# A hybrid mLSTM / gMLP layer on one core: the second pair of output projection tiles as seven block products, with the work around it moved between engines

## Chip, cores and metric

The kernel runs on one core of a Trainium2 chip. The metric is device time in microseconds (us) of one execution. One execution is also profiled; its span, from the first to the last instruction, is the clock of all rows below.

## The reference, cut to what matters

There is one layer. The token count is 520: 512 of a prompt and 8 single tokens of samples. The model width is 1024 and the hidden width 2816.

```
xn = rmsnorm(x, g1);  z = xn @ w_in                  # q, k, v, o, gates, u, vb, ga, gb
y_a = (sigmoid(o) * mlstm(q, k, v, ig, lf)) @ w_a    # recurrence over 4 chunks of 128 tokens, 4 heads
y_b = spatial_gate(gelu(u), rmsnorm(gelu(vb))) @ w_b
merged = sigmoid(ga) * y_a + sigmoid(gb) * y_b
x = x + merged @ w_o                                 # x1: the output projection, called WO here
xn = rmsnorm(x, g2)                                  # needs the sum of x1's squares
up = xn @ w_up;  conv over 3 rows;  x = x + (silu(a) * gval) @ w_down;  rmsnorm(x, g_final)
```

## The kernel before, in words

**Tiles and slots.** Activations lie feature-major: 128 features on the partitions, 520 tokens in the row, `KT` = 8 feature blocks. A weight slot is 1024 by 128, which gives one output tile of 128 features. Slots are numbered in the order in which they are used; `S_WO` is the first of the 8 slots of the output projection, `S_UP` follows, then `S_DN`. Two buffers of each kind (`raw`, `whi`, `wlo`, and the output banks `out_ps`) are used by even and odd slots in turn.

**Each product is made of three.** Every fp32 operand is split in a high part, which fp32r holds exactly, and a low part, the rest. For a weight slot SyncE loads `raw`, ScalarE copies it to `whi` (`split`, line 581 through the helper `A`), VectorE subtracts to get `wlo` (`low`, L1083), and TensorE multiplies whi by x high, whi by x low and wlo by x high. With 8 blocks of the inner dimension and two halves of 260 tokens (`HALF`) that is 48 matmuls a slot. `split` of slot c waits until slot c-2 is done, since it overwrites that slot's `whi`.

**Seven products for eight.** In some places two output tiles are calculated as a 2 by 2 block product: two inner halves, two halves of the tokens. Seven products of 12 matmuls each (`product`) take the place of eight. This needs sums of weight blocks (`weight_sums`, lines 1497 to 1502: four VectorE operations in two dependent steps), seven factors split by `factor_hi` on ScalarE and `factor_low` on VectorE (L1491), and four combinations of the activations (0 to 3), split the same way (`x_combination_hi` on ScalarE, `x_combination_low` on VectorE, L1430). The factors are, in order, a11, a12, wsum3, wsum1, wsum0, wsum2, a22, so the third product (number 2, after 0 and 1) is the first that needs the weight sums. Before the change five pairs of gate tiles (`pairs_w`) and three pairs of the down projection (`pairs_d`) do this. In the gate pairs the first four factors of the next pair are prepared while two ordinary tiles (`n2`, `n3`) run between pairs. The combinations of x for the gate pairs are made by VectorE with `x_sum` (L1421) and `x_difference` (L1425): two of the sums in the last two steps of the recurrence (m = 6 and 7), the rest right behind it.

**The output projection.** After the last gate pair, 8 tiles follow, `S_WO` to `S_WO + 7`. For each, VectorE adds the residual `xres` (L1605, one operand in PSUM) to get `x1[j]`, ScalarE makes `x2h`, VectorE `x2l` (L1610). GpSimd loads `xres` and the convolution's constants by DMA, prepares the samples' share of the convolution (`sconv`, lines 1926 to 1931, behind a DMA that writes `conv_old`), and then squares each `x1[j]` (L1936) and adds it to `acc` (L1938). TensorE sums `acc` over the partitions (`norm_sums`) in the midst of tile `S_UP`, after its sixth of eight steps.

**Order.** Each engine runs its own list of instructions in the order in which they are written. Nothing reorders them. Waits are on semaphores, and a waiting instruction holds up all behind it on its engine.

Of the kernel before, what the change touches and what calls it, by code (L numbers as in the profile page):

```python
# [86 lines left out]
def hybrid_layer(nc, ins, outs):  # L87
    with ExitStack() as ctx:
# [92 lines left out]
        assert 16800 + 3 * NH * DVA * 4 >= XB + 3 * XB // 4  # L181
        acth = at("acth", [P, FT, TOK], Q0, F32R)
# [54 lines left out]
        sqa = st("sqa", [P, TOK], 2080)  # L237

# [55 lines left out]
        class DownPair(Pair):  # L294


            def __init__(self, i):
                self.q = GATE_PAIRS + i
# [14 lines left out]
        pairs_d = [DownPair(i) for i in range(DOWN_PAIRS)]  # L313
        pairs_w = [Pair(q) for q in range(GATE_PAIRS)]
# [104 lines left out]
        s_dc = sem("down_product_copied")  # L419
        s_nh = sem("branch_half_hi")  # L420
# [4 lines left out]
        s_acc = sem("norm2_sums")  # L425
        s_ss2 = sem("norm2_broadcast")
# [39 lines left out]
        def _(sp):  # L466
# [70 lines left out]
            load_slots(S_WO, S_DN)  # L537
# [41 lines left out]
        def _(act):  # L579
# [280 lines left out]

            def next_factors_hi(pr):
# [27 lines left out]
            def ay_pair(pr):  # L889
# [28 lines left out]
                if last:  # L918
                    split(At(S_WO + 1))
                else:  # L920
# [10 lines left out]
            with act.Fori(0, KT // 2) as i:  # L931
                for t in range(2):
                    n = At(S_WO + t, i, 2)
                    split(n.plus(2))
                    apart()
                    act.wait_ge(s_x1, i * 2 + (t + 1))
                    A(x2h[:, i * 2 + t, :], x1[:, i * 2 + t, :], scale=gains[:, 2, bass.ds(i * 2 + t, 1)]).then_inc(s_x2h, 1)


# [44 lines left out]
            def down_combination_hi(r, src, at):  # L984

                act.wait_ge(s_bt, 4 + at)
# [89 lines left out]
        def _(dve):  # L1076
# [378 lines left out]
            for m in range(2 * NC):  # L1455
# [12 lines left out]
                unit_denominator(2 * m + 1)  # L1468
                if m == 6:
                    x_sum(0, 0, 0)  # L1470
                if m == 7:
                    x_sum(1, 0, 1)
# [30 lines left out]

            def first_gate_sum(pr):
# [38 lines left out]
            def ay_pair(pr):  # L1543
# [28 lines left out]
                if last:  # L1572
                    low(At(S_WO))
                    merged_low(pr.j)
# [24 lines left out]
            def wo_step(i):  # L1599

                for t in range(2):
                    n = At(S_WO + t, i, 2)
                    j = i * 2 + t
                    ready(n)
                    TT(both(x1[:, j, :]), out2(n), both(xres[:, j, :]), ALU.add).then_inc(evac[n.c % 2], 1)  # L1605
                    dve.drain()
                    dve.nop().then_inc(s_x1, 1)
                    low(n.plus(2))
                    dve.wait_ge(s_x2h, i * 2 + (t + 1))
                    STT(x2l[:, j, :], x1[:, j, :], gains[:, 2, bass.ds(j, 1)], x2h[:, j, :].bitcast(F32),  # L1610
                        ALU.mult, ALU.subtract).then_inc(s_x2, 1)

            dve.wait_ge(s_xres, 16)
            wo_step(0)
            dve.wait_ge(s_xrest, 16)
            with dve.Fori(1, KT // 2) as i:
                wo_step(i)
# [82 lines left out]
            def down_combination_low(r, src, at):  # L1700

                dve.wait_ge(s_th, 4 + at)
# [121 lines left out]
        def _(pool):  # L1824
# [93 lines left out]
            pool.dma_start(xres[:, 2:KT, :], ins["x_all"][:, 2:KT, :]).then_inc(s_xrest, 16)  # L1918
            pool.wait_ge(done, S_WO + 1)
            pool.dma_start(cst[:, :, :, :], ins["conv_state"]).then_inc(s_ffl, 16)  # L1920
            pool.dma_start(cwb[:, :, :], ins["conv_wb"]).then_inc(s_ffl, 16)
            pool.wait_ge(s_ffl, 32)
# [9 lines left out]
            pool.memset(acc[:, :], 0.0)  # L1932
            pool.drain()
            for j in range(KT):
                pool.wait_ge(s_x1, j + 1)
                pool.tensor_tensor(sqa[:, :], x1[:, j, :], x1[:, j, :], ALU.mult)  # L1936
                pool.drain()  # L1937
                pool.tensor_tensor(acc[:, :], acc[:, :], sqa[:, :], ALU.add)  # L1938
                pool.drain()  # L1939
# [19 lines left out]
        def _(pe):  # L1959
# [254 lines left out]
            def branch_tile(pr, hi, lo):  # L2214
# [14 lines left out]
            for pr in pairs_w:  # L2229
# [4 lines left out]
                branch_tile(pr, *branches)  # L2234
# [4 lines left out]
            with pe.Fori(1, 4) as i:  # L2239
                for t in range(2):  # L2240
                    tile(At(S_WO + t, i, 2), mh, ml)
# [51 lines left out]
            def down_pair(pr):  # L2293
# [12 lines left out]
                pe.wait_ge(s_tl, 4 + 2)  # L2306
                product(pr, 3, pr.p6, *down_combination(2)).then_inc(s_pd, 1)
                product(pr, 4, pr.p5, *down_combination(0)).then_inc(s_pd, 1)
                pe.wait_ge(s_tl, 4 + 3)
                product(pr, 5, pr.p7, *down_combination(1)).then_inc(s_pd, 1)  # L2310
                pe.wait_ge(s_tl, 4 + 4)
# [137 lines left out]
```

## Time and profile before

| | |
|---|---|
| median of 3 runs | 898.91 us (898.21 to 899.29) |
| the profiled execution | 898.24 us, its span 896.4 us |
| granted TensorE clock, mean | 0.997 of full |
| TensorE matmul busy | 887.7 us, 99% |
| VectorE / ScalarE / GpSimd busy | 68% / 44% / 15% |

TensorE is busy nearly all the time, so what it does sets the time. The other engines prepare its operands. Their shares are averages; what matters is whether each operand is ready when TensorE comes to it.

### The profile page before, as it was taken

To read this page: it belongs to the slowest core of one execution; us is meant where nothing else is said; L and a number is where in the kernel's file an instruction comes from. 1 tells how busy PE (TensorE), PEld (TensorE's weight loads), DVE (VectorE), ACT (ScalarE), POOL (GpSimd) and SP (SyncE) were. 2 spreads that over 40 slices of the span, in tenths; PEclk is the share of its full clock that TensorE was granted. 3 is DMA by queue.
4 is the path that set the end of the run, shared out by engine and by line. 5 is a ranking of instruction groups with operands and counts; after the bars stand their busy time and mean duration, and the time that the engine had idled before them with its cause. 6 is when DMAs were issued, how large, how long until landed. Compare 5 with 4: busy or idle time off the path is not lost.

```text
span 896.4 us, 18963 instructions
## 1 busy us (share of the span) xinstructions
PE 887.7 (99%) x7306; PEld 883.2 (99%) x7306; DVE 609.7 (68%) x980; ACT 390.5 (44%) x629; POOL 133.0 (15%) x182
## 2 busy tenths in 40 slices
PE   9999999999999999999999999999999999999997
PEld 8999999999999999999999999999999999999997
DVE  7895775442885568677755777777777778966544
ACT  7535434544864334344432344444444444433334
POOL 0673000002542110000005700000000000000001
PEclk9999999999999999999999999999999999999998
DMA  6332253234872222322255222222222222333232
GB/s 214 114 123 94 72 202 99 78 99 155 280 269 72 71 72 75 115 95 94 95 200 136 83 82 94 94 94 94 94 88 82 87 94 88 99 107 88 89 106 96
DMA packets 31499, 100.44 MB, mean 112 GB/s; under 512 B 4668, under 2 KB 7260, under 8 KB 31192
## 3 DMA queue, kind: packets, MB, share of 16 engines
q1 hardware_dynamic: 29256, 92.96, 31.2%
q0 software_dynamic: 1472, 5.72, 2.2%
q10 hardware_dynamic: 720, 1.04, 0.4%
q8 instruction: 36, 0.59, 0.3%
q14 instruction: 15, 0.12, 0.0%
HBM read 92.37 MB, written 7.35 MB: 111 GB/s over the span
## 4 chain that ended last, share of the span: by engine, by line
PE 88%; issue 3%; POOLq 3%; DMA 2%; DVE 2%; POOL 1%; ACT 0%; DVEq 0%; SPq 0%; ACTq 0%
PE out L1961 81%; PE trp L1961 3%; PE aux L1961 2%; POOLq L1939 2%; POOLq L1937 1%; DMA raw_pair<-in_w_slots 1%; PE trp L1995 1%; DMA cwb<-in_conv_wb 1%; PE aux L2153 0%; DVE wlo L1083 0%; DVE tf L1425 0%; DVE tl L1430 0%; POOL y L1952 0%; DVE tf L1421 0%; POOL out_conv_old L1923 0%
## 5 line engine op out<-in xcount | busy, mean ns | idle before, releaser
L581 ACT ACTIVATE whi<-raw_pair 128x1024 fp32r<-128x1024 f32 (+4 forms) x168 | 154.2, 924 | 210.3 <-PE out L1961 196.4
L1083 DVE TENSOR_TENSOR wlo<-raw_pair,whi 128x1024 fp32r<-128x1024 f32 (+1 forms) x121 | 154.0, 1273 | 89.6 <-ACT whi L581 89.2
L1961 PE MATMUL out<-xh,whi 128*128 128x260 f32 x668 | 143.4, 289 | 0.4 <-DVE wlo L1491 0.4
L1961 PE MATMUL out<-x2h,wlo 128*128 128x260 f32 x704 | 141.9, 283 | 0.0
L1961 PE MATMUL out<-x2h,whi 128*128 128x260 f32 x704 | 141.8, 282 | 0.0
L1961 PE MATMUL out<-x2l,whi 128*128 128x260 f32 x704 | 141.7, 283 | 0.0
L1961 PE MATMUL out<-xl,whi 128*128 128x260 f32 x668 | 139.3, 283 | 0.0
L1961 PE MATMUL out<-xh,wlo 128*128 128x260 f32 x668 | 139.2, 283 | 0.0
L1961 PEld LDWEIGHTS out<-x2h,whi 128*128 128x128 f32 x704 | 108.6, 188 | 0.1
L1961 PEld LDWEIGHTS out<-x2h,wlo 128*128 128x128 f32 x704 | 108.5, 188 | 0.0
L1961 PEld LDWEIGHTS out<-x2l,whi 128*128 128x128 f32 x704 | 108.2, 188 | 0.0
L1961 PEld LDWEIGHTS out<-xh,whi 128*128 128x128 f32 x668 | 105.4, 189 | 1.0 <-issue 0.6
L1961 PEld LDWEIGHTS out<-xh,wlo 128*128 128x128 f32 x668 | 105.0, 188 | 0.0
L1961 PEld LDWEIGHTS out<-xl,whi 128*128 128x128 f32 x668 | 104.9, 188 | 0.0
L1961 PE MATMUL out<-acth,whi 128*128 128x260 f32 (+2 forms) x266 | 58.2, 283 | 0.0
L1961 PE MATMUL out<-acth,wlo 128*128 128x260 f32 (+2 forms) x266 | 58.0, 283 | 0.0
L1961 PE MATMUL out<-actl,whi 128*128 128x260 f32 (+2 forms) x266 | 57.9, 283 | 0.0
L1645 DVE TENSOR_TENSOR up<-out,rbc 128x520 f32<-128x520 f32 x44 | 30.8, 701 | 38.9 <-PE out L1961 38.8
L1945 POOL COPY nconv<-up 128x10 f32 x44 | 10.4, 236 | 241.4 <-DVEq L1646 241.4
L581 ACT ACTIVATE acth<-silu 128x520 f32 (+1 forms) x22 | 14.1, 639 | 69.8 <-DVE silu L1660 69.8
L1961 PEld LDWEIGHTS out<-acth,whi 128*128 128x128 f32 x266 | 42.8, 188 | 0.1
L1961 PEld LDWEIGHTS out<-acth,wlo 128*128 128x128 f32 x266 | 42.8, 188 | 0.0
(362 smaller groups left out, 1755.8 us busy)
## 6 DMA issues: line engine op xcount, KB each, us to landing
raw_pair<-in_w_slots SPq DMA_DIRECT2D x123, 512.0 KB, 3.3
raw_pair<-in_w_dn SPq DMA_DIRECT2D x16, 448.0 KB, 3.4
c_ring<-in_C_state SPq DMA_DIRECT2D x8, 512.0 KB, 5.4
row<-scratch SPq DMA_DIRECT2D x8, 512.0 KB, 5.7
out_C_sample<-c_ring SPq DMA_DIRECT2D x8, 512.0 KB, 4.9
raw_pair<-in_w_dn SPq DMA_DIRECT2D x8, 512.0 KB, 3.5
xres<-in_x_all POOLq DMA_DIRECT2D x1, 1560.0 KB, 6.9
x<-in_x_all SPq DMA_DIRECT2D x5, 260.0 KB, 6.8
```

Of the source, the lines that this page charges most:

```text
L581: return act.activation(out, in_, func, **kw_)
L1083: TT(wlo[p][:, 0:width], raw[p][:, 0:width], whi[p][:, 0:width].bitcast(F32), ALU.subtract)\
L1645: TT(both(up[t][:, 2:2 + TOK]), out2(n), both(rbc2[:, :]), ALU.mult).then_inc(evac[n.c % 2], 1)
L1937: pool.drain()
L1939: pool.drain()
L1945: pool.tensor_copy(nconv[:, i * 2 + t, :], up[t][:, SEQ:2 + TOK]).then_inc(s_nc, 1)
L1961: return pe.matmul(*a, **k)
L1995: m = pe.transpose(trp[b.c % 2][:, c, :], ftmp[b.c % 2][:, c * P:(c + 1) * P], ident[:, :])
```

## The change

1. **OutPair.** Output tiles `j` = 2 and 3 become a pair of seven products, between tile `S_WO + 1` and tile `S_WO + 4`. Its slot `S_WO + 4` is loaded and split in halves, as a gate pair's third slot is. The four combinations are of `merged`, whose last two of eight tiles come from the last gate pair.
2. **x's combinations** move: the sums to steps 4, 5 and 6 of the recurrence, three differences to steps 6 and 7.
3. **Squares** of x1 are made by ScalarE (`second_square`) into two buffers in turn; GpSimd only adds them. A square waits until the square two before it has been added.
4. **GpSimd's conv preparation** comes behind the first four additions, ahead of the last four.

The diff, cut to its core (the gpsimd block is told whole; the DMA order and the buffers are left out where they only follow):

```diff
@@ VectorE, in the recurrence
+                if m == 4: x_sum(0, 0, 0)
+                if m == 5: x_sum(1, 0, 1)
                 if m == 6:
-                    x_sum(0, 0, 0)
+                    x_sum(2, KT // 2, 1)
+                    x_difference(0, 1, 0)
                 if m == 7:
-                    x_sum(1, 0, 1)
+                    x_difference(1, 2, 1)
+                    x_difference(2, 2, 0)
@@ VectorE, behind the recurrence (by_plain, i == NC)
-                    x_difference(0, 1, 0)
                     unit_low(NC * NH - 1)
-                    x_sum(2, KT // 2, 1)
-                    dve.drain()
-                    x_difference(1, 2, 1)
-                    x_difference(2, 2, 0)
@@ VectorE, last gate pair
                     low(At(S_WO))
+                    merged_difference(0, merged_quarter(0, 1), merged_quarter(0, 0))
                     merged_low(pr.j)
@@ VectorE, the output projection (wo_step for all j before)
+            def out_pair(pr):
+                ready(At(S_WO)); first_sum(At(S_WO), 0); first_result()
+                merged_combination_low(0, 1)
+                merged_combination_low(2, 2)
+                factor_low(pr, 0)
+                factor_low(pr, 1)
+                weight_sums(pr)
+                ready(At(S_WO + 1)); first_sum(At(S_WO + 1), 1); first_result()
+                factor_low(pr, 2)
+                second_low(0)
+                factor_low(pr, 3)
+                merged_combination_low(1, 3)
+                factor_low(pr, 4)
+                factor_low(pr, 5)
+                merged_combination_low(3, 4)
+                second_low(1)
+                dve.wait_ge(s_xrest, 16); dve.wait_ge(s_pd, 6 * q + 3)
+                first_sum(n[0], j)
+                factor_low(pr, 6)
+                ...
+                TT(part(0, 1), part(0, 1), wtmp[1], ALU.add)
+                first_result()
+                low(n[3])
+                ready(n[1])
+                TT(part(1, 0), rest(0), wtmp[0], ALU.add)
+                TT(part(1, 1), rest(1), wtmp[0], ALU.add)
+                dve.drain()
+                TT(part(1, 0), part(1, 0), out_ps[pr.t1][:, 0, 0:HALF], ALU.add).then_inc(evac[pr.t1], 1)
+                ...
+            dve.drain()
+            merged_difference(2, merged_quarter(1, 1), tf[:, 0, :, :])
+            merged_difference(1, merged_quarter(1, 1), merged_quarter(0, 1))
+            dve.drain()
+            merged_difference(3, merged_quarter(1, 0), tf[:, 2, :, :])
+            out_pair(pair_o)
@@ ScalarE
+            def second_square(j):
+                act.wait_ge(s_x1a, j + 1)
+                A((ftmp[1], ftmp2)[j % 2][:, :], x1[:, j, :], ACT.Square).then_inc(s_x1q, 1)
+            def out_pair(pr):
+                factor_hi(pr, 0); factor_hi(pr, 1)
+                second_hi(0); second_square(0)
+                act.wait_ge(s_sw, 4 * q + 4); act.wait_ge(done, n[1]())
+                factor_hi(pr, 2); factor_hi(pr, 3)
+                ...
+                split(n[3])
+                second_square(1)
+            merged_combination_hi(2, 2); merged_combination_hi(1, 3); merged_combination_hi(3, 4)
+            out_pair(pair_o)
+            second_hi(2); second_square(2); second_hi(3); second_square(3)
+            for j in range(4, KT):
+                split(At(S_WO + j + 2)); second_hi(j); second_square(j)
@@ SyncE
-            load_slots(S_WO, S_DN)
+            load_slots(S_WO, S_WO + 4)
+            (S_WO + 4 once the pair's weight sums and two low factors are made, S_WO + 5 once all seven are)
+            load_slots(S_WO + 6, S_DN)
@@ GpSimd
+            pool.memset(acc[:, :], 0.0); pool.drain()
+            for j in range(4): square_added(j)      # wait for the square, acc += square, drain
             (DMA of conv_old, four tensor operations of the conv preparation)
-            for j in range(KT): (wait for x1[j], sqa = x1 * x1, drain, acc += sqa, drain)
+            for j in range(4, KT): square_added(j)
@@ TensorE
-            with pe.Fori(1, 4) as i:  (tiles S_WO + 2 to S_WO + 7)
+            out_pair(pair_o)                        # products 0 to 6, 12 matmuls each
+            halves_tile(pair_o, mh, ml)             # S_WO + 4
+            for j in range(5, KT): tile(At(S_WO + j), mh, ml)
```

## Rows read from the trace of the kernel before

**Rows 1.** The page, busy time of the engines.
```profile
PE 887.7 (99%) x7306; PEld 883.2 (99%) x7306; DVE 609.7 (68%) x980; ACT 390.5 (44%) x629; POOL 133.0 (15%) x182
```
**Rows 2.** The chain that ended last: start, us, what.
```profile
46.71 5.77 PE out L1961 x48
...
349.21 4.76 DMA raw_pair<-in_w_slots
```
**Rows 3.** Timeline of TensorE: start, us, line, operation, count, idle before.
```profile
357.87 0.28 PE L1961 MATMUL out<-xh,wlo 128*128 128x260 f32 x1
358.52 0.35 PE L1961 MATMUL out<-xh,whi 128*128 128x260 f32 x1 [0.37 <-DVE wlo L1491]
...
463.72 0.40 PE L1961 MATMUL out<-mh,whi 128*128 128x260 f32 x2
...
475.25 0.40 PE L1961 MATMUL out<-mh,whi 128*128 128x260 f32 x2
```
**Rows 4.** Timeline of VectorE: a combination, the weight sums, two factors.
```profile
342.58 1.24 DVE L1430 TENSOR_TENSOR tl<-tf,th 128x1040 fp32r<-128x1040 f32 x1
...
373.66 0.68 DVE L1497 TENSOR_TENSOR wsum<-raw_pair 128x512 f32<-128x512 f32 x1
...
375.82 0.69 DVE L1502 TENSOR_TENSOR wsum<-raw_pair,wsum 128x512 f32<-128x512 f32 x1
...
378.16 1.29 DVE L1491 TENSOR_TENSOR wlo<-wsum,whi 128x512 fp32r<-128x512 f32 x2
```
**Rows 5.** Timeline of ScalarE: a combination's high part, two factors, mh, x2h.
```profile
337.61 1.08 ACT L581 ACTIVATE th<-tf 128x1040 fp32r<-128x1040 f32 x1 [2.47 <-DVE tf L1425]
...
377.49 1.15 ACT L581 ACTIVATE whi<-wsum 128x512 fp32r<-128x512 f32 x2 [4.55 <-PE out L1961]
...
465.44 0.64 ACT L581 ACTIVATE mh<-merged 128x520 fp32r<-128x520 f32 x1 [0.40 <-DVE merged L1481]
...
470.75 0.73 ACT L581 ACTIVATE x2h<-x,gains  x1
```
**Rows 6.** Timeline of VectorE at the start of the output projection.
```profile
465.33 1.22 DVE L1083 TENSOR_TENSOR wlo<-raw_pair,whi 128x1024 fp32r<-128x1024 f32 x1
466.46 0.69 DVE L1486 TENSOR_TENSOR ml<-merged,mh 128x520 fp32r<-128x520 f32 x1
469.75 0.70 DVE L1605 TENSOR_TENSOR x<-out,xres 128x520 f32<-128x520 f32 x1 [2.60 <-PE out L1961]
...
471.93 0.75 DVE L1610 SCALAR_TENSOR_TENSOR x2l<-x,gains,x2h 128x520 fp32r<-128x520 f32 x1
```
**Rows 7.** Timeline of VectorE and GpSimd together, 487 to 492 us.
```profile
487.43 1.32 POOL L1938 TENSOR_TENSOR acc<-acc,sqa 128x520 f32<-128x520 f32 x1
488.08 1.74 DVE L1083 TENSOR_TENSOR wlo<-raw_pair,whi 128x1024 fp32r<-128x1024 f32 x1 [0.27 <-ACT whi L581]
...
488.88 1.85 POOL L1936 TENSOR_TENSOR sqa<-x 128x520 f32<-128x520 f32 x1
489.75 1.55 DVE L1610 SCALAR_TENSOR_TENSOR x2l<-x,gains,x2h  x1
```
**Rows 8.** Weight loads of the output projection (SyncE), time from issue to landing.
```profile
DMA to landing us min/median/max: 3.1/3.3/6.7
```
**Rows 9.** Timeline of GpSimd: the convolution's preparation, and the last sum of squares.
```profile
473.41 2.07 POOL L1923 DMA_DIRECT2D out_conv_old<-cst  x1 [7.63 <-DMA cwb<-in_conv_wb]
...
483.18 1.07 POOL L1929 TENSOR_TENSOR sconv<-sconv,cwb 128x352 f32<-128x352 f32 x1 [6.01 <-issue]
484.41 1.21 POOL L1931 TENSOR_TENSOR sconv<-sconv,sct 128x352 f32<-128x352 f32 x1
...
512.20 2.11 POOL L1938 TENSOR_TENSOR acc<-acc,sqa 128x520 f32<-128x520 f32 x1
```
**Rows 10.** Timeline of TensorE around the sum over the partitions in tile S_UP.
```profile
513.93 0.41 PE L1961 MATMUL out<-x2h,wlo 128*128 128x260 f32 x2
514.41 1.14 PE L1961 MATMUL aux<-acc,ones 128*128 128x260 f32 x4
```

More of the change, by code:

```diff
@@ L313, in hybrid_layer, with __init__ @@
         pairs_d = [DownPair(i) for i in range(DOWN_PAIRS)]
+        class OutPair(Pair):
+            def __init__(self):
+                self.q = GATE_PAIRS
+                self.j = 2
+                self.n = [At(S_WO + 2 + t) for t in range(4)]
+                self.t0, self.t1 = self.n[0].c % 2, self.n[1].c % 2
+                self.p1, self.p6 = (trp[t][:, :, :].rearrange("p a b -> p (a b)")[:, 0:HALF] for t in range(2))
+                self.p5, self.p7 = (aux[:, t, 0:HALF] for t in range(2))
+                r0, r1 = raw[self.t0], raw[self.t1]
+                self.a11, self.a12, self.a21, self.a22 = r0[:, 0:HW], r0[:, HW:], r1[:, 0:HW], r1[:, HW:]
+                self.factor = (self.a11, self.a12, wsum[:, 3, :], wsum[:, 1, :], wsum[:, 0, :], wsum[:, 2, :], self.a22)
+        pair_o = OutPair()
+        wtmp = (ftmp[0][:, 0:HALF], ftmp[0][:, HALF:TOK])
         pairs_w = [Pair(q) for q in range(GATE_PAIRS)]
@@ L425, in hybrid_layer @@
         s_acc = sem("norm2_sums")
+        s_x1q = sem("x1_squared")
+        s_x1a = sem("x1_squares_summed")
         s_ss2 = sem("norm2_broadcast")
@@ L928, in _, with second_hi @@
                 ay_pair(pr)
[L931 to L937, printed above, removed]
+            def second_hi(j):
+                act.wait_ge(s_x1, j + 1)
+                A(x2h[:, j, :], x1[:, j, :], scale=gains[:, 2, j:j + 1]).then_inc(s_x2h, 1)
@@ L940, in up_step @@
+            merged_combination_hi(2, 2)
+            merged_combination_hi(1, 3)
+            merged_combination_hi(3, 4)
+            out_pair(pair_o)
+            second_hi(2)
+            second_square(2)
+            second_hi(3)
+            second_square(3)
+            for j in range(4, KT):
+                split(At(S_WO + j + 2))
+                second_hi(j)
+                second_square(j)
             def up_step(i, first=False, last=False):
@@ L1597, in _ @@
                 ay_pair(pr)
[L1599 to L1611, printed above, removed]
@@ L1613, in _, with second_low, first_sum @@
-            dve.wait_ge(s_xres, 16)
[L1614 to L1617, printed above, removed]
+            def second_low(j):
+                dve.wait_ge(s_x2h, j + 1)
+                STT(x2l[:, j, :], x1[:, j, :], gains[:, 2, j:j + 1], x2h[:, j, :].bitcast(F32),
+                    ALU.mult, ALU.subtract).then_inc(s_x2, 1)
+            def first_sum(n, j):
+                return TT(both(x1[:, j, :]), out2(n), both(xres[:, j, :]), ALU.add).then_inc(evac[n.c % 2], 1)
@@ new lines, in _ @@
+            dve.drain()
+            merged_difference(2, merged_quarter(1, 1), tf[:, 0, :, :])
+            merged_difference(1, merged_quarter(1, 1), merged_quarter(0, 1))
+            dve.drain()
+            merged_difference(3, merged_quarter(1, 0), tf[:, 2, :, :])
+            dve.wait_ge(s_xres, 16)
+            out_pair(pair_o)
+            for j in range(4, KT):
+                n = At(S_WO + j)
+                ready(n)
+                first_sum(n, j)
+                first_result()
+                low(n.plus(2))
+                second_low(j)
@@ L1921, in _ @@
             pool.dma_start(cwb[:, :, :], ins["conv_wb"]).then_inc(s_ffl, 16)
+            pool.memset(acc[:, :], 0.0)
+            pool.drain()
+            for j in range(4):
+                square_added(j)
             pool.wait_ge(s_ffl, 32)
@@ L1931, in _ @@
             pool.tensor_tensor(sconv[:, :, :], sconv[:, :, :], sct[:, :, :], ALU.add).then_inc(s_scv, 1)
[L1932 to L1939, printed above, removed]
+            for j in range(4, KT):
+                square_added(j)
             pool.nop().then_inc(s_acc, 1)
```

126 lines of the change are left out of this document (115 added, 11 removed).

## The prediction

> **What bounds the kernel now.** I read the page first, for shares: TensorE's matmuls fill 99% of the span, the other engines far less [rows 1]. So the time is that of a list of matmuls at a fixed pace, plus whatever stalls TensorE has. The chain of waits gives the pace: 48 matmuls in 5.77 us, which is 0.120 us each [rows 2]. The timeline of TensorE then shows where the pace breaks near the places that the change touches. Ahead of product 2 of the first gate pair the distance between two starts is 358.52 - 357.87 = 0.65 us in place of 0.12, a stall of 0.53, put down to a weight factor's low part on VectorE [rows 3]. Ahead of the sum of squares in tile S_UP it is 514.41 - 513.93 = 0.48 us for the 0.24 of a group of two, a stall of 0.24, and GpSimd's last addition ended at 512.20 + 2.11 = 514.31 [rows 9, 10]. Through the output projection there is no stall: the first tile starts at 463.72 and the third at 475.25 [rows 3], 11.53 us or twice 5.77, and the six that follow go on so. The reader is to see that the change has little to win there. All it can take away is matmuls and these two stalls, while it puts work on VectorE in a place where each slot needs few VectorE operations.
>
> **What it takes away.** Two tiles are 96 matmuls, seven products 84. Twelve at 0.120 us are 1.44 us. In the recurrence, the moved operations start from the chain's row in which a weight load was issued only at 349.21 and took 4.76 us to land [rows 2]; the weight sums, and with them product 2, waited for it. The change takes four operations of 1.24 us [rows 4] out of the VectorE work ahead of this load, so it comes some 2 us earlier, and the stall of 0.53 goes. What is late next is the factor's high part on ScalarE, which can start only when the tile before the pair is done; in the second gate pair the first of these low parts started at 378.16 [rows 4], two factors' high parts having started at 377.49 [rows 5], and TensorE ran through. I take the whole 0.53. Within the recurrence the moved work costs nothing: in the steps m = 6 and 7 one operation more, 1.15 us, or two of them stand ahead of the gating of a unit, and TensorE needs that result only for the transpose of the next unit, four steps of its tiles (5.77 us for eight), or 2.9 us, later. If this cover were gone, it would cost up to 1.2 us in each of the two.
>
> **The pair, step by step.** Between operations of VectorE that wait for nothing, the next starts 0.09 us before the end of the one before (465.33 + 1.22 against 466.46 [rows 6]); behind a drain I add 0.10.
> - *Before the first product.* ScalarE makes one combination's high part (1.08 [rows 5]) ahead of the last tile of merged, so VectorE's low part of it ends at about 467.25, not 467.15 [rows 6]. TensorE wants it at 468.8: no stall.
> - Then come three differences of merged that need its last tile: 3 x 1.24 less overlap, with two drains, to 471.1. The first sum x1 (0.70 [rows 6]) to 471.8. Two low parts of combinations (1.24 each [rows 4]) to 474.1. Factor 0's low part (1.29 for two, 0.69 for one [rows 4]) to 474.7; product 0 is due at 475.25 [rows 3], in time.
> - *GpSimd steps in.* ScalarE's list is three high parts of combinations, to 472.2, two factors, x2h (0.73 [rows 5]), and the square (0.64, as for mh [rows 5]): done at 474.5. GpSimd's addition starts then. How the two engines get on is in the rows: GpSimd's addition ran from 487.43 to 488.75, and VectorE's low part, begun at 488.08, took 1.74 [rows 7] where it takes 1.22 alone [rows 6]; GpSimd's square ran from 488.88 to 490.73, and VectorE's x2l, begun at 489.75, took 1.55 [rows 7] where it takes 0.75 alone [rows 6]. The extra is each time what was left of GpSimd's operation, less 0.15: the later one waits for the earlier. An addition of 1.31 costs VectorE about 1.0 here: factor 1's low part ends at 476.3.
> - *Weight sums.* 373.66 to 376.51 is 2.85 us [rows 4]: done at 479.1. ScalarE waits for them, then makes factor 2's high part (0.63) to 479.7. VectorE adds x1 of the second tile in between, to 479.8, then factor 2's low part to 480.5. TensorE starts 0.13 later, at 480.6. Product 2 is due at 475.25 + 2.88 = 478.15. **Stall 2.45.** Without GpSimd it would be 1.47.
> - *Products 3 to 6.* VectorE has behind this x2l, factor 3, combination 1, factor 4: 0.66 + 0.60 + 1.15 + 0.60, which is 0.13 more than products 2 and 3. Then factor 5, combination 3, x2l, x1 of the third tile, factor 6, which is 0.74 too late for product 6. **Stalls 0.13 and 0.74.** Product 6 starts at 487.2, ends at 488.7.
> - *Behind the pair.* The load of slot S_WO + 5 is issued when factor 6 is done, 487.1. With the median of 3.3 us [rows 8] it lands at 490.5, is split on ScalarE to 491.6, and has its low part at 492.9. ScalarE then releases GpSimd's second addition, which takes VectorE's next operation away until it has ended, and the bank that tile S_WO + 5 writes is empty only at 495.1. The tile is due at 488.7 + 5.77 = 494.45. **Stall 0.75.**
>
> The pair's stalls are 2.45 + 0.13 + 0.74 + 0.75 = 4.07 us.
>
> **Squares and conv preparation.** The last of x1's first four tiles is complete at 495.5, its addition at 498.2. The preparation took 485.62 - 473.41 = 12.2 us before [rows 9], 6.0 of them a gap in front of a tensor operation for which the profile names no releaser. Taken as it was, with about 1.1 for VectorE beside it, it ends at 511.7. Four additions of 1.31 to 2.1 us follow, and the sixth square waits for the first of them: the last ends at 518.1. TensorE reaches the sum at 495.20 + 3 x 5.77 + 4.33 = 516.84. **Stall 1.43**, where before it was 0.24: 1.19 more. If the gap is shorter by 1.5 us, this is nothing and even the 0.24 goes. The other end is a gap of 8 us, which makes the stall 2.5.
>
> **Sum.** -1.44 - 0.53 + 4.07 + 1.19 = +3.3 us. The profiled execution took 898.24, so it would take 901.5; the median is 0.67 above it, so I predict 902.2 for the median.
>
> The low end: without any hindrance by GpSimd the pair stalls 1.47 + 0.13 + 0.74 = 2.34, the other two not at all: -1.44 - 0.53 - 0.24 + 2.34 = +0.1, or 899.0. The high end: the load of S_WO + 5 at 5 us and not 3.3 (the slowest of these took 6.7 [rows 8]) adds 1.7, a longer gap 1.0: 904.8.
>
> What these rows show is a wait, not a sharing of speed. The Trainium skill says the same (SBUF — State Buffer, Who interferes with whom): a VectorE instruction with two SBUF inputs and a GpSimd instruction that reads SBUF exclude each other for the whole instruction, and one with an operand in PSUM is free. By that rule the trace agrees: the addition of x1 from PSUM took 0.70 with or without GpSimd. It speaks against this change, since nearly all that it gives VectorE has both inputs in SBUF; a proportional slowdown would give about the same sum.
>
> **Rivals.** A difference of 0.2% (1.8 us) is about what a measurement of this kernel can tell from no change.
> - *A: the pair is fed too late, as above,* +3.3 us, 902.2. For it: the order of the lists is fixed, and 2.85 us of weight sums stand between factor 1 and factor 2. Chance 0.58.
> - *B: the same places, but small,* between -1.8 and +1.8, most likely near +0.5: GpSimd's additions fall into VectorE's waits, the gap shrinks when its DMA runs on an idle queue. For it: VectorE was slowed by GpSimd at 488 and 489 [rows 7], and TensorE had no stall there. Against it: in those tiles VectorE had time to spare, such as the 2.60 us ahead of the first x1 [rows 6]; in the pair it has none. Chance 0.24.
> - *C: it ends on the other side.* VectorE is ready with factor 2 when product 2 is due. Gain 1.44 + 0.53 + 0.24 = 2.2 us, 896.7. The gate pairs do this, with their weight sums made ahead of the pair. It decides at one point: factor 2's low part must be complete by 478.0, 2.45 us sooner than I count. Chance 0.10, of which 0.06 beyond 0.2%.
> - *D: GpSimd becomes the bound of the sum of squares* or the late load of S_WO + 5 lasts as the slowest did: +5 to +7, 904 to 906. Half of the slow DMA's reason, the transfer of xres beside it, is over by then. Chance 0.08.
>
> The range goes from 899.0 to 904.8: it leaves out C, the lower part of B, and the upper part of D, 0.19 in all. Faster by over 0.2%: C's 0.06 and 0.01 of B, 0.07. Within 0.2%: 0.27. Slower: 0.66. The likeliest case alone has 900.9 to 903.7.
>
> **What would show it.** In the profile after: TensorE 12 matmuls fewer, and an idle stretch of 2.4 us (over 1.4 at least) ahead of the third product, at about 478 less the 0.5 of the earlier gain, put down to VectorE's line of factor_low; smaller ones ahead of products 4 and 6. No stall at 358. VectorE busy without a break from 463 to 487. A factor's low part of nearly 1.7 us beside the first addition of GpSimd. At the sum of squares a wait for GpSimd of 1 to 1.5 us, with the conv preparation ending behind 510. I would be wrong if product 2 starts on time, if GpSimd's addition does not delay VectorE there, or if the preparation's gap is gone. The mean granted clock before was 0.997 of full; if an idle stretch of 2.4 us lowers it, the matmuls behind it would take longer than I count, which I take as nothing.

## The result, and the profile after

The changed kernel takes 903.32 us (median of 5 runs, 902.74 to 903.38); the kernel before took 898.91 beside it (5 runs, 898.21 to 899.29). The ratio is 1.0052, with a 95% interval of 1.0040 to 1.0063: slower by 4.4 us. The profiled execution took 902.74, with a span of 901.0, 4.6 above the span before (896.4).

The page, busy time of the engines (after):
```profile
PE 888.7 (99%) x7294; PEld 883.9 (98%) x7294; DVE 625.2 (69%) x1006; ACT 400.3 (44%) x648; POOL 122.6 (14%) x174
```
The list is shorter by twelve matmuls, 7,294 for 7,306 [rows 1], and yet TensorE is busy 1.0 us longer. A matmul list that shrinks while its busy time grows is a first sign of a slower pace, not only of waits.

Timeline of TensorE, after (start, us, operation, and in brackets the idle time before it):
```profile
463.22 0.40 PE L2125 MATMUL out<-mh,whi 128*128 128x260 f32 x2
...
474.75 0.28 PE L2125 MATMUL trp<-mh,whi 128*128 128x260 f32 x1
...
477.58 0.28 PE L2125 MATMUL out<-mh,wlo 128*128 128x260 f32 x1
480.30 0.58 PE L2125 MATMUL out<-mh,whi 128*128 128x260 f32 x1 [2.44 <-DVE wlo L1575]
480.68 0.42 PE L2125 MATMUL out<-ml,whi 128*128 128x260 f32 x1
480.89 0.42 PE L2125 MATMUL out<-mh,wlo 128*128 128x260 f32 x1
...
483.49 0.33 PE L2125 MATMUL trp<-mth,wlo 128*128 128x260 f32 x1
483.66 0.28 PE L2125 MATMUL trp<-mth,whi 128*128 128x260 f32 x1
...
489.09 0.41 PE L2125 MATMUL out<-mh,whi 128*128 128x260 f32 x2
...
496.17 0.47 PE L2125 MATMUL out<-mh,whi 128*128 128x260 f32 x2 [1.15 <-DVE x L1757]
...
519.00 1.14 PE L2125 MATMUL aux<-acc,ones 128*128 128x260 f32 x4 [0.97 <-POOLq L2082]
```
The row at 463.72 before [rows 3] is now at 463.22. The pair runs from 474.75 to 489.09, 14.34 us for 84 matmuls that need 84 x 0.120 = 10.08. Of the 4.26 lost, 480.30 - 477.58 - 0.12 = 2.60 stand ahead of product 2. The rest is in the next rows: behind the stall two starts lie 0.21 us apart, and from 483.66 on 0.12 again.

Stretches of TensorE, after (from and to, length, busy time and count for TensorE, weight loads, VectorE, ScalarE and GpSimd, then the granted clock, the DMA share, GB/s):
```profile
479.00:480.00 1.00, 0.00 (x0) 0.00 (x0) 0.86 (x2) 1.00 (x3) 0.00 (x0) 1.00 0.24 45
480.00:481.00 1.00, 0.70 (x3) 0.71 (x4) 1.00 (x3) 1.00 (x2) 0.00 (x0) 0.58 0.91 324
481.00:482.00 1.00, 1.00 (x7) 1.00 (x7) 1.00 (x2) 0.92 (x3) 0.00 (x0) 0.50 0.39 156
482.00:483.00 1.00, 1.00 (x6) 1.00 (x6) 1.00 (x2) 0.00 (x0) 0.00 (x0) 0.50 0.00 0
483.00:484.00 1.00, 1.00 (x8) 1.00 (x7) 1.00 (x3) 0.64 (x1) 0.00 (x0) 0.71 0.00 0
484.00:485.00 1.00, 1.00 (x11) 1.00 (x10) 1.00 (x2) 0.00 (x0) 0.00 (x0) 1.00 0.00 0
```
The granted clock is 0.50 of full, 1.2 GHz and not 2.4, from about 480.2, just ahead of the restart, to 483.6. Products 2 to 6 take 489.09 - 480.30 = 8.79 us for 60 x 0.120 = 7.20, so 1.59 are lost there, 1.56 of them by 483.66. A slower TensorE asks for its factors later, so the stalls forecast ahead of products 4 and 6 don't show.

Timeline of VectorE, after:
```profile
471.32 2.39 DVE L1599 TENSOR_TENSOR tl<-tf,mth 128x1040 fp32r<-128x1040 f32 x2
473.63 2.40 DVE L1575 TENSOR_TENSOR wlo<-raw_pair,whi 128x512 fp32r<-128x512 f32 x2
475.96 0.68 DVE L1581 TENSOR_TENSOR wsum<-raw_pair 128x512 f32<-128x512 f32 x1
...
479.55 0.69 DVE L1575 TENSOR_TENSOR wlo<-wsum,whi 128x512 fp32r<-128x512 f32 x1
...
492.53 1.53 DVE L1754 TENSOR_TENSOR x<-xres,ftmp 128x260 f32<-128x260 f32 x1
493.99 1.53 DVE L1755 TENSOR_TENSOR x<-xres,ftmp 128x260 f32<-128x260 f32 x1
495.60 0.43 DVE L1757 TENSOR_TENSOR x<-x,out 128x260 f32<-128x260 f32 x1
...
497.86 0.69 DVE L1701 TENSOR_TENSOR x<-out,xres 128x520 f32<-128x520 f32 x1
```
Timeline of GpSimd, after:
```profile
473.96 1.52 POOL L2081 TENSOR_TENSOR acc<-acc,ftmp 128x520 f32<-128x520 f32 x1 [8.12 <-ACT ftmp L610]
491.96 1.81 POOL L2081 TENSOR_TENSOR acc<-acc,ftmp 128x520 f32<-128x520 f32 x1 [16.48 <-ACT ftmp L610]
493.94 1.30 POOL L2081 TENSOR_TENSOR acc<-acc,ftmp 128x520 f32<-128x520 f32 x1 [0.16 <-issue]
497.76 1.36 POOL L2081 TENSOR_TENSOR acc<-acc,ftmp 128x520 f32<-128x520 f32 x1 [2.52 <-ACT ftmp L610]
499.77 2.09 POOL L2093 DMA_DIRECT2D out_conv_old<-cst  x1 [0.65 <-issue]
...
502.61 0.95 POOL L2097 TENSOR_TENSOR sct<-cst,cwb 128x352 f32<-128x352 f32 x1
509.87 1.21 POOL L2099 TENSOR_TENSOR sconv<-sconv,cwb 128x352 f32<-128x352 f32 x1 [6.31 <-issue]
...
516.82 2.06 POOL L2081 TENSOR_TENSOR acc<-acc,ftmp 128x520 f32<-128x520 f32 x1 [0.16 <-issue]
```
Read the two side by side. Two low parts of factors take 2.40 beside the addition at 473.96 and 1.29 alone [rows 4]. The two halves of x take 1.53 each beside the additions at 491.96 and 493.94, where the same operation takes 0.43 in the mended kernel, with no addition beside it:
```profile
488.52 0.43 DVE L1758 TENSOR_TENSOR x<-xres,ftmp 128x260 f32<-128x260 f32 x1 [0.18 <-issue]
```
And x1 from PSUM, at 497.86, takes its usual 0.69 within the addition at 497.76. From 474 to 488 VectorE is busy 13.59 of 14.00 us; before it was 6.99 of the same stretch.

### The profile page after: what moved, and what is told of

It reads as the page before. It is cut to its first block, busy times and chain, and to the rows that moved or that the text cites. A ratio compares the mean times of both kernels' runs of the same rounds, so it can differ in the third digit from the quotient of the medians.

```text
span 901.0 us, 18890 instructions
## 1 busy us (share of the span) xinstructions
PE 888.7 (99%) x7294; PEld 883.9 (98%) x7294; DVE 625.2 (69%) x1006; ACT 400.3 (44%) x648; POOL 122.6 (14%) x174
## 4 chain that ended last, share of the span: by engine, by line
PE 89%; issue 7%; POOLq 2%; POOL 1%; DMA 0%; ACT 0%; SPq 0%; ACTq 0%
PE out L2125 82%; PE trp L2125 3%; PE aux L2125 2%; POOLq L2082 1%; PE trp L2159 1%; DMA raw_pair<-in_w_slots 0%; PE aux L2317 0%; POOL y L2116 0%; POOL out_conv_old L2093 0%; ACT xg L610 0%; POOLq L2100 0%; POOL sconv L2101 0%; POOLq L88 0%; ACT whi_last L610 0%; POOLq L2098 0%
## 5 line engine op out<-in xcount | busy, mean ns | idle before, releaser
L610 ACT ACTIVATE whi<-raw_pair 128x1024 fp32r<-128x1024 f32 (+3 forms) x170 | 154.0, 913 | 196.4 <-PE out L2125 179.1
L1161 DVE TENSOR_TENSOR wlo<-raw_pair,whi 128x1024 fp32r<-128x1024 f32 (+1 forms) x118 | 150.1, 1272 | 90.4 <-ACT whi L610 89.9
```

What stands on the lines that cost most here:

```text
L610: return act.activation(out, in_, func, **kw_)
L1161: TT(wlo[p][:, 0:width], raw[p][:, 0:width], whi[p][:, 0:width].bitcast(F32), ALU.subtract)\
```

## Experiments

Every kernel was compared with the kernel before on its own chip. In the first four that one took 898.62 (21 runs), in the next four 898.43 (27), in the next two 898.76 (15), then 898.78 and 898.73.

**The change without the pair.** Before, plus x's combinations in the recurrence, squares on ScalarE, and the conv preparation behind four additions.
```diff
-                    TT(sqa, x1[:, j], x1[:, j])  TT(acc, acc, sqa)   # GpSimd, eight times
+                    A(ftmp, x1[:, j], Square)                        # ScalarE; GpSimd adds only
```


> The kernel before with all of the change but the pair: x's combinations within the recurrence, squares on ScalarE, the conv preparation behind four additions. Theory (the pair's late operands, and what follows from them, are the loss): 0.3 to 0.8 us faster than before, because the stall of 0.5 us ahead of the first gate pair's product 2 goes and the one at the sum of squares is at most 0.5. Rival 1 (the moves are the loss, the conv preparation's place above all): 1 us or more slower than before, with a wait of over 1 us for GpSimd at the sum of squares. Here x1's first four tiles come evenly, so the preparation should begin some 4 us ahead of where it began in the changed kernel relative to tile S_UP.


Measured: 898.28, ratio 0.9997 (0.9988 to 1.0006), span 896.1. The stall at the gate pair is gone, and the sum of squares waits 0.21. So these three parts cost nothing by themselves: the median is 0.3 below, and the interval reaches from 1.1 faster to 0.5 slower. The loss needs the pair.

**The first four squares later.**
```diff
-                second_square(0)   # and (1), (2), (3), inside and behind the pair
+            for j in range(4):     # behind second_hi(3)
+                second_square(j)
```


> The changed kernel with the squares 0 to 3 put behind x2h of tile 3 on ScalarE's list, so that GpSimd adds nothing while VectorE feeds the pair. Theory (GpSimd's additions hold VectorE up): the stall ahead of product 2 falls from 2.6 to about 1.5 us, the one ahead of tile S_WO + 5 from 1.3 to under 0.3; the sum of squares waits longer, by 2 to 4 us, since the preparation begins later. In all about the time of the changed kernel. If the low clock of 1.5 us behind the stall depends on the length of the stall, it is gone. Rival (VectorE is late for its own list alone): the stalls at product 2 and at S_WO + 5 stay within 0.3 us of 2.6 and 1.3.


Measured: 904.14, 1.0058 (1.0043 to 1.0073). With no addition in the pair the stall ahead of product 2 falls from 2.60 to 1.54, which is the 1.47 of the prediction's list without GpSimd. But the four squares now stand together ahead of a split on ScalarE and wait for GpSimd's additions; the slot is late and TensorE stalls 2.51 ahead of tile S_WO + 6. The stall ahead of S_WO + 5 is gone, the clock stays full, and the wait for the sum of squares is 1.76, only 0.6 more, not 2 to 4. The wait moved. (The profiled execution of this kernel was 1.8 us late already at the row that stands at 46.64 in the changed kernel, so its stalls can be compared, and its span can't.)

**The DMA of conv_old behind everything.**
```diff
-            pool.dma_start(outs["conv_old"], ...)   # ahead of the conv preparation
+            pool.dma_start(outs["conv_old"], ...)   # behind the last addition
```


> The changed kernel with the DMA of conv_old issued behind all additions in place of ahead of the conv preparation. Theory A (the gap of 6.3 us inside the preparation is GpSimd's drain waiting for this DMA): the gap is under 0.5 us, the preparation takes some 4.5 us and not 12.7, and the wait of 1.0 us for GpSimd at the sum of squares is gone; 0.8 to 1.2 us faster than the changed kernel. Theory B (the gap belongs to the tensor operations themselves): it stays at about 6 us and so does the wait.


Measured: 902.43, 1.0047 (1.0032 to 1.0063). GpSimd's timeline in this kernel:
```profile
499.83 1.63 POOL L2095 TENSOR_TENSOR sconv<-cst,cwb 128x352 f32<-128x352 f32 x1 [0.16 <-issue]
501.42 1.31 POOL L2096 TENSOR_TENSOR sct<-cst,cwb 128x352 f32<-128x352 f32 x1
502.88 0.86 POOL L2098 TENSOR_TENSOR sconv<-sconv,cwb 128x352 f32<-128x352 f32 x1
503.88 0.95 POOL L2100 TENSOR_TENSOR sconv<-sconv,sct 128x352 f32<-128x352 f32 x1
```
The gap of 6 us is gone: the four operations take 5.0 us from first to last, not 512.44 - 501.80 = 10.6. The gap stood between the second and the third, where the code has a drain, and came only with GpSimd's own DMA just issued. The wait for the sum of squares falls from 1.14 to 0.21, and the median is 0.9 below that of the changed kernel, though in another set of runs. The stall ahead of product 2 is 2.60, as before this edit, and the one ahead of S_WO + 5 is 1.56.

**VectorE's list in another order,** with the two edits above: combinations and x2l behind the factors.
```diff
-                merged_combination_low(0, 1); merged_combination_low(2, 2)
                 factor_low(pr, 0); factor_low(pr, 1)
+                merged_combination_low(2, 2)
                 weight_sums(pr)
-                factor_low(pr, 2); second_low(0); factor_low(pr, 3); merged_combination_low(1, 3)
+                factor_low(pr, 2); factor_low(pr, 3); merged_combination_low(0, 2)
```


> The changed kernel with VectorE's and ScalarE's lists reordered: factors 0 and 1 ahead of the combinations, the weight sums as soon as their load has landed, combination 0 behind factor 3, both x2l of the first tiles behind the pair, the bank of S_WO + 5 emptied ahead of that slot's low part; with the late squares and the late conv_old DMA too. Theory (only the order was at fault): product 2 waits under 0.4 us, products 3 to 6 together under 0.6, nothing behind, full clock: 1.3 to 2.0 us faster than before, 897.0 to 897.6. Rival 1 (VectorE has too much work for the pair in any order): the stall only moves to products 4 to 6 and is 1.5 us or more; then not faster than before. Rival 2 (products in seven are slow in themselves): 84 matmuls take more than 0.125 us each even without a wait.


Measured: 900.81, 1.0020 (1.0011 to 1.0029). Product 2 waits 0.40. The gain that I expected is not there. The loss is now one stall of 2.20 ahead of tile S_WO + 5, since the low part of its slot stands behind two x2l and beside an addition (2.31 us for 1.23). The granted clock then falls to 0.50 from 495.5 to 498.9, which costs another 1.6.

**The order mended.** That low part ahead of the two x2l, weight sum 3, which factor 2 needs, ahead of weight sum 2, x1 of the second tile behind factor 3's low part, and the squares spread over the last four tiles.
```diff
+                low(n[3])
                 second_low(0); second_low(1)
-                low(n[3])
+            squares = {4: (0, 1), 5: (2, 3), 6: (4, 5, 6), 7: (7,)}
```


> As the reordered run, and with what it showed mended: slot S_WO + 5's low part ahead of the two x2l, the squares of tiles 0 to 7 spread over the last four tiles on ScalarE, weight sum 3 ahead of weight sum 2, the second tile's x1 behind factor 3. Theory (the loss is the order, nothing in the seven products): waits in and behind the pair under 0.3 us together, the wait at the sum of squares as before at 0.2, full clock throughout: -1.44 - 0.5 + 0.2 = 1.7 us faster than before. Rival (each cure moves the wait): another wait of 1 us or more in tiles S_WO + 4 to S_UP, and not faster than before.


Measured: 898.61, 1.0005 (0.9996 to 1.0014). No stall ahead of product 2 nor of S_WO + 5, 0.62 us in three small waits inside the pair, full clock. Yet it ties, where I expected 1.7 less. What is left is one row of TensorE, 1.60 late:
```profile
514.97 1.14 PE L2132 MATMUL aux<-acc,ones 128*128 128x260 f32 x4 [1.43 <-POOLq L2089]
```
**The old order with the spread squares.** VectorE's list is that of the changed kernel.


> The changed kernel's own order for the pair, but with the squares spread over the last four tiles and the conv_old DMA behind all additions, so that GpSimd does nothing beside the pair and no wait for it is left. Theory: the stalls are those of VectorE's list alone, 1.5 ahead of product 2 and 0.7 to 0.8 ahead of product 6, none ahead of S_WO + 5, full clock: -1.44 - 0.5 + 2.4 = 0.5 us slower than before, 4 us faster than the changed kernel. Rival (what GpSimd does there hardly matters): within 1.5 us of the changed kernel.


Measured: 900.37, 1.0023 (1.0014 to 1.0032): 1.55 ahead of product 2 and 0.74 ahead of product 6, full clock, and 1.57 at the sum of squares, which I had not expected. So it is 1.9 slower than before and not 0.5, and 3.0 faster than the changed kernel and not 4. Against the mended order it is 1.76 slower: the price of the order of VectorE's and ScalarE's lists alone.

**The changed kernel once more,** one run.


> The changed kernel once more, for its profile. If the low clock is the regular answer to the stall of 2.6 us, it is seen again, 3 to 3.4 us long, costing 1.4 to 1.7 us; the waits themselves stay within 0.1 of 2.6, 1.3 and 1.1.


Measured: 903.52, span 901.8. Timeline of TensorE:
```profile
480.66 0.39 PE L2125 MATMUL out<-mh,whi 128*128 128x260 f32 x1 [2.43 <-DVE wlo L1575]
...
487.41 0.36 PE L2125 MATMUL out<-mth,whi 128*128 128x260 f32 x1 [0.57 <-DVE wlo L1575]
...
496.68 0.48 PE L2125 MATMUL out<-mh,whi 128*128 128x260 f32 x2 [1.81 <-DVE x L1757]
```
Its stretch behind the first stall (columns as above):
```profile
481.00:482.00 1.00, 1.00 (x11) 1.00 (x10) 1.00 (x3) 1.00 (x3) 0.00 (x0) 1.00 0.82 328
```
The stall ahead of product 2 is the same, 2.59, but the clock stays full. The 0.73 ahead of product 6 is then there, and tile S_WO + 5 waits 1.98 in place of 1.31. What it waits for comes at VectorE's pace and from a load that the last factor releases, whatever TensorE's clock: it starts 496.68 - 480.66 = 16.02 us behind product 2 here, and 496.17 - 480.30 = 15.87 with the low clock. The low clock and these stalls stand in for each other, and by these two profiles the total is about the same either way.

**One square early,** in the mended order: square 0 inside the pair.
```diff
                 second_hi(0)
+                second_square(0)
```


> The run with the fixed order, but the square of tile 0 back at its early place, so that one addition of GpSimd (1.3 us) falls into the pair. Theory (an addition holds VectorE up for its whole length, and here VectorE has no slack): 0.6 to 1.3 us of new stalls in the pair, 0.6 to 1.3 us slower than the fixed order. Rival (lock only matters in the late order): under 0.3.


Measured: 899.85, 1.0018 (1.0008 to 1.0027), 1.24 slower than the mended order. VectorE in the mended order:
```profile
473.97 0.68 DVE L1719 TENSOR_TENSOR wsum<-raw_pair 128x512 f32<-128x512 f32 x1
```
VectorE in this kernel:
```profile
474.04 1.79 DVE L1720 TENSOR_TENSOR wsum<-raw_pair 128x512 f32<-128x512 f32 x1
```
And GpSimd:
```profile
473.91 1.38 POOL L2089 TENSOR_TENSOR acc<-acc,ftmp 128x520 f32<-128x520 f32 x1 [7.71 <-ACT ftmp L610]
```
One addition begun 0.13 us ahead of VectorE takes 1.11 us from it, and the pair's waits grow from 0.62 to 1.64. This is the cleanest measurement of what such an addition costs here.

**Squares sooner.** Squares 0 and 1 right behind the split of x of tile 3, in the mended order.
```diff
-            squares = {4: (0, 1), 5: (2, 3), 6: (4, 5, 6), 7: (7,)}
+            second_square(0); second_square(1)
+            squares = {4: (2, 3), 5: (4,), 6: (5, 6), 7: (7,)}
```


> The kernel of e5_fixed_order with tile 3's eight squares given to ScalarE about one tile earlier each (squares 0 and 1 right behind the split of x of tile 3, the others spread over tiles S_WO+4 to S_WO+7), so that GpSimd's additions end before TensorE asks for the sum of squares. Theory (the pair now costs about 0.6 us of waits, and what is left of the loss in e5_fixed_order is the 1.6 us wait for the sum of squares): that wait falls to about 0.2, the pair's waits stay at 0.6, and the time is 1.44 + 0.5 - 0.6 = about 1.3 us below the kernel before, that is near 897.2 where before is at 898.5. Rival 1 (an addition of GpSimd that falls into the pair costs TensorE as much as the early square of e8_early_square did, 1.0 us): the wait for the sum goes and the pair loses 1.6, so that the time is within 0.5 us of before. Rival 2 (the additions are late for another reason, the conv preparation ahead of them): the wait stays at 1.2 or more and the time ties with before.


Measured: 898.78, 0.9999 (0.9990 to 1.0008). The wait for the sum falls from 1.60 to 0.31, but the two additions from 491.76 to 495.28 stretch VectorE's four x2l from 2.77 to 4.89, the low part behind them is late, and TensorE stalls 0.79 ahead of tile S_WO + 6. Rival 1 has the time right, a tie, but not the place: the pair's waits stay at 0.6, and the loss stands behind it.

**The pair with GpSimd's old work.** The changed kernel, its squares and conv preparation as before the change.
```diff
-            for j in range(4): square_added(j)       # ahead of the conv preparation
+            for j in range(KT):                      # behind it
+                TT(sqa, x1[:, j], x1[:, j]); TT(acc, acc, sqa)
```


> Two parts of the change alone: the pair of tiles in seven products and x's combinations inside the recurrence; the squares of tile 3 are GpSimd's again and its conv preparation stands where it did before. Theory (what TensorE loses in the pair is VectorE's lateness, and each operation of GpSimd that reads SBUF beside VectorE's two-input operations adds to it): before, GpSimd computes at 473 to 477 and at 483 to 492, so VectorE is held up more than in the changed kernel, the stall ahead of product 2 is 3 us or more, tile S_WO+5 still waits about 1, and the sum of squares about 0.3; the time is 902.5 to 904.5. Rival (GpSimd's place does not matter, the order of VectorE's list alone makes the stalls): product 2 waits 2.5 as in the changed kernel, the sum of squares 0.3, and the time is about 1 us below the changed kernel, near 901.5 or less.


Measured: 908.90, 1.0105 (1.0090 to 1.0121). Both theories fall short: mine by 4.4 us at least, the rival by more. TensorE in this kernel:
```profile
482.08 0.58 PE L2122 MATMUL out<-mh,whi 128*128 128x260 f32 x1 [3.85 <-DVE wlo L1570]
...
494.09 0.36 PE L2122 MATMUL out<-mth,whi 128*128 128x260 f32 x1 [3.25 <-DVE wlo L1570]
```
And VectorE:
```profile
475.94 2.48 DVE L1576 TENSOR_TENSOR wsum<-raw_pair 128x512 f32<-128x512 f32 x1
...
485.78 3.25 DVE L1570 TENSOR_TENSOR wlo<-wsum,whi 128x512 fp32r<-128x512 f32 x2
```
I had priced GpSimd's work ahead of product 2 and of S_WO + 5 only. GpSimd's squares and additions from 485.37 to 492.18 hold VectorE too (3.25 for what takes 1.29), so product 6 waits another 3.41, and the low clock comes twice, from 480.8 to 487.6 and from 494.4 to 497.8. Without the pair the same two parts are within the 0.3 us of the first experiment, by its interval 1.1 at most; with it, 908.90 - 903.32 = 5.6. They are what keeps the pair's loss small.

**The conv preparation behind all additions,** in the mended order.
```diff
-            for j in range(4): square_added(j)
+            for j in range(KT): square_added(j)
             (conv preparation, 4 operations)
-            for j in range(4, KT): square_added(j)
```


> The kernel of e5_fixed_order with GpSimd's conv preparation (0.86, 0.86, 1.66 and 1.23 us there, 4.8 from first to last) behind all eight additions of squares instead of between the fourth and the fifth. In e5_fixed_order the fifth addition began at 508.38 though its square was there at about 506, and the last one ended at 514.84, which made the wait of 1.43 us for the sum of squares. Theory (that wait is all that is left of the loss, and the preparation makes it): the additions five to seven run at 503.6, 505 and about 507 to 510, the last one starts when its square is done, at about 512.5, and ends at 514 or just after; the sum of squares waits 0.2 to 0.7 instead of 1.43, the pair's waits stay, and the time is 0.7 to 1.1 below that of e5_fixed_order, that is 897.4 to 897.9 where before is at 898.5. The preparation then runs at about 514 to 519 and is first needed at 522. Rival (the last addition is late because VectorE's split of a slot beside it holds it up to 2.1 us, wherever the preparation is): the wait stays over 1 us and the time stays at 898.6, a tie with before.


Measured: 898.57, 1.0000 (0.9991 to 1.0009). The sum of squares starts on time, at 513.25, yet against the kernel before nothing is won. TensorE stalls 0.98 further on:
```profile
522.31 0.50 PE L2130 MATMUL out<-x2h,whi 128*128 128x260 f32 x2 [0.81 <-DVE up L1811]
```
VectorE:
```profile
516.98 3.40 DVE L1805 RECIPROCAL rbc<-rbc 128x520 f32<-128x520 f32 x1 [3.67 <-issue]
```
GpSimd:
```profile
515.98 0.95 POOL L2108 TENSOR_TENSOR sconv<-sconv,sct 128x352 f32<-128x352 f32 x1
```
The reciprocal's input was complete at 515.03. It starts at 516.98, 0.05 us after GpSimd's last operation ends: VectorE waits for the preparation ahead of the reciprocal, for the sake of two memsets into storage that the preparation still uses. The row puts this wait down to "issue". Neither theory had it.

**That wait behind the reciprocal.**
```diff
-                        dve.memset(up[0][:, 0:2], 0.0); dve.memset(up[1][:, 0:2], 0.0)
                         dve.wait_ge(s_std2, 1)
                         dve.reciprocal(rbc2[:, :], rbc2[:, :])
                         low(n.plus(2))
+                        dve.wait_ge(s_scv, 1)
+                        dve.memset(up[0][:, 0:2], 0.0); dve.memset(up[1][:, 0:2], 0.0)
...
-            dve.wait_ge(s_scv, 1)
             up_step(0, True)
```


> The kernel of e11_prep_last with VectorE's wait for the conv preparation, and the two memsets that need it, moved from ahead of the reciprocal of the norm to behind it and the split after it. In e11_prep_last the sum of squares came on time (513.25, stall 0.0) but the reciprocal began at 516.98, right when the last operation of the preparation ended (516.93), though its input was complete at 515.03; TensorE then stalled 0.98 us ahead of the second tile of slots at 522.31. Theory (that stall is the late reciprocal alone): the reciprocal begins at about 515.2, TensorE has no stall at 522, and the span falls by about 1.0 us below that of e11_prep_last, that is to about 895.2; the median is near 897.6, or 1.0 to 1.4 below before (ratio 0.9985 to 0.999). Rival (something else behind it is late by as much, since the reciprocal or the split would then run beside GpSimd's preparation, which ends at 517): the stall stays at 0.5 us or more, and the time is again within 0.5 us of before.


Measured: 897.07 (11 runs, 896.80 to 898.30) beside 898.73, ratio 0.9985 (0.9976 to 0.9994), span 895.4. TensorE:
```profile
513.47 1.04 PE L2130 MATMUL aux<-acc,ones 128*128 128x260 f32 x4
...
520.83 0.40 PE L2130 MATMUL out<-x2h,whi 128*128 128x260 f32 x2
```
VectorE:
```profile
515.28 3.40 DVE L1803 RECIPROCAL rbc<-rbc 128x520 f32<-128x520 f32 x1 [1.74 <-ACT rbc L610]
```
The reciprocal starts when its input is there and the stall at 522 is gone. This is the one version that is clearly faster than both kernels: by the medians 1.7 us under before (0.5 to 2.2 by the interval), 6.2 under the changed kernel. It has the twelve matmuls less, and no wait over 0.25 us from the pair to the up projection. Not all of the 1.7 is the pair's: without it the median was already 0.3 under before.

## Why the prediction was right, and where it was off

The direction, the place and the mechanism were right (rival A), and the median of 903.32 lies in the range, 1.1 above the forecast. By its own terms, from the profiled executions:

| term | predicted | measured |
|---|---|---|
| twelve matmuls | -1.44 | -1.44 |
| stall in the first gate pair | -0.53 | gone; -0.50 (the output projection starts 0.50 earlier) |
| ahead of product 2 | +2.45 | +2.60 |
| products 2 to 6 | +0.87 | +1.59 |
| ahead of S_WO + 5 | +0.75 | +1.31 |
| sum of squares, beyond the 0.24 before | +1.19 | +0.90 |
| sum | +3.3 | +4.5 (the spans: +4.6) |

- *Product 2.* The order of VectorE's list makes 1.54 of it, measured with no addition in the pair (1.47 predicted); the addition beside it makes the other 1.06 (0.98 predicted). Taking both away ends the stall: shown.
- *The waiting of VectorE for GpSimd* is a wait for the rest of the other's operation, as predicted from [rows 7]: 1.11 us for one addition in two different kernels, in the second of them with 473.91 + 1.38 - 474.04 = 1.25 left of it. The Trainium skill (SBUF — State Buffer, Who interferes with whom) calls it an exclusive lock between a VectorE instruction with two inputs in SBUF and a GpSimd instruction that reads SBUF. By that rule the rows after agree, 2.40 for 1.29, and 0.69 for the operation from PSUM.
- *Products 2 to 6.* The prediction says of the clock: "if an idle stretch of 2.4 us lowers it, the matmuls behind it would take longer than I count, which I take as nothing". It was 1.59 for the five products, in the place of the forecast stalls of 0.13 and 0.74. This is the largest difference in the table, but not what made the sum too small. Tile S_WO + 5 starts 15.87 us behind product 2 with the low clock and 16.02 in the repeat with the full one, so a right guess of the clock would have changed next to nothing. This row and the next are to be read together: +1.62 predicted, +2.90 measured, and 16.02 - 108 x 0.120 = 3.06 in the repeat.
- *S_WO + 5* is then the mis-sized step that matters most; its mechanism is right. "GpSimd's second addition, which takes VectorE's next operation away": there were two additions, 0.17 us apart, and each took one operation, 1.10 us over its 0.43. I had counted only the first. The other is most of the 1.28 by which the two rows together fall short. With the squares later, the two operations took 0.42 each and this stall was gone.
- *Sum of squares.* "Taken as it was": the preparation took 12.7 us with a gap of 6.3, and the wait was 1.14, a little less than the 1.43. The profile names no releaser for the gap; the run with the DMA moved shows that the DMA just ahead makes it. Why it lasts as long as it does is not shown.
- *The moved combinations* cost nothing in the recurrence, and the stall at 358 is gone in every kernel that has them: the first pair's weight sums begin at 351.26, at 354.06 before. The profiled executions differ by up to 1.8 us in the time at which the first tiles run, so the gain is read from a row near the start. From 46.71 [rows 2] to 463.72 [rows 3] are 417.01 us before, and 463.22 - 46.64 = 416.58 in the changed kernel. In eleven of the twelve experiments' profiles it is 416.52 to 416.58, in one (squares sooner) 416.80. So this part is worth 0.43 to 0.49, close to the forecast 0.53, and 0.21 in the one.
- *Rival B* was wrong for this kernel. The mended order has the time that it names, but another reason: product 2 is not late there. *Rival C* is what the last experiment reaches, except that -2.2 becomes -1.7: 0.5 to 0.6 of small waits remain in the pair.

What stays open: why the low clock follows one stall and not another of the same length, and how the last 0.1 to 0.5 us of each sum divide (in the profiled executions the first 50 us and the last 25 differ by as much, and in one by more).

## What to carry to other kernels

Trading matmuls for VectorE work pays only if VectorE's list is ordered by when TensorE asks, and the other engines' work is placed around it: the same seven products came with a loss of 4.4 us in one arrangement and a gain of 1.7 in another, and 1.76 of that is the order of VectorE's and ScalarE's lists alone. Where VectorE has no slack, a GpSimd operation beside one with both inputs in SBUF is paid nearly in full (1.1 us for one of 1.4), so move GpSimd's SBUF work out of such a stretch, and look at what the move pushes behind it. Parts of a change are not additive: the moved squares and conv preparation were worth next to nothing alone and 5.6 us beside the pair. And a stretch that looks expensive, such as the slow clock here, costs nothing if TensorE has to wait behind it for something else.

## What the runs showed of the hardware

- **The granted clock fell with stalls that are short,** but not regularly. Stalls of 2.60 (the changed kernel, just ahead of the restart), 2.60 again (conv_old's DMA moved, 1.5 us after TensorE had resumed), 2.20 (the first reordering, 1.5 us after), 3.41 (0.3 us after) and 4.01 (already inside the stall) came with 0.50 of full, 1.2 GHz, for about 3.4 us, or 6.8 in the last case. A stall of 2.59 of the same kernel, and ones of 2.51, 1.98, 1.76 and less, came with none. One such stretch of 3.4 us made the matmuls in it take about 1.6 us longer.
- **GpSimd's operations behind a drain came 4 to 7 us late when its own DMA had just been issued:** 6.31 and, in the repeat, 6.59 us, 5.91 with the late squares, 4.56 without the pair, 4.38 with the pair and the old GpSimd work, and 6.01 before, with no releaser named; gone in every kernel that issues the DMA last.
- **A wait for GpSimd's signal can stand as "issue"** on VectorE's row (3.67 at 516.98). What ends at that moment on another engine tells more than the name.
